# Expert routing formed tile by tile inside the output projection, and the last down weights split into another buffer

## The reference, cut to what matters

```python
x = x + merged @ w_o
h = rms_norm(x, norm2_g)
g_logits = h @ w_group_router + b_group_router      # 4 groups
e_logits = h @ w_expert_router + b_expert_router    # 4 x 8 experts
grp = argmax(g_logits); top_val, top_idx = top_k(e_logits[grp], 2)
gates = softmax(g_logits)[grp] * softmax(top_val)
# tokens sorted by expert, each expert's list padded to blocks of 128 rows
y_block = (silu(xb @ w_gate[e]) * (xb @ w_up[e])) @ w_down[e]
x = x + gates[0] * y[first] + gates[1] * y[second]
y_out = rms_norm(x, final_norm_g)
```

## Time and profile before

| | us |
|---|---|
| median of 3 runs | 1621.45 (1621.17 to 1624.1) |
| the profiled execution, its own time | 1620.94 |
| its span | 1619.1 |
| TensorE busy in the span | 1495.6 (92%) |
| VectorE busy | 931.2 (58%) |
| ScalarE busy | 796.5 (49%) |
| GpSimd busy | 384.5 (24%) |
| the chain that ended last: TensorE | 40% |

### The profile page before, as it was taken

One profiled execution on the slowest core, in us unless ns is written; L12 is line 12 of the kernel. 1 busy time (PEld: TensorE's weight loads), 2 busy tenths in 40 slices (PEclk: granted clock), 3 DMA queues, 4 the chain that ended last, 5 costly groups with the idle time before them and its releaser, 6 DMA issues. The chain is left out here.

```text
span 1619.1 us, 26480 instructions
## 1 busy us (share of the span) xinstructions
PE 1495.6 (92%) x8989; PEld 1316.9 (81%) x8990; DVE 931.2 (58%) x1017; ACT 796.5 (49%) x1040; POOL 384.5 (24%) x403
## 2 busy tenths in 40 slices
PE   5899999999999999998993499999999999999964
PEld 5798998899999899997882388888888888888851
DVE  4415323622335345474336588898886676679836
ACT  4217415712932222551113078878876575677833
POOL 0370073046042000000004333332332222232210
PEclk9999999999999999999996699999999999999987
DMA  6211221232162663464623289999996696699948
GB/s 207 77 62 37 67 81 48 68 93 80 47 220 77 206 134 118 156 207 139 210 92 114 74 313 366 367 380 378 378 389 244 252 385 252 235 366 377 359 174 318
DMA packets 165361, 329.94 MB, mean 204 GB/s; under 512 B 17022, under 2 KB 62376, under 8 KB 164776
## 3 DMA queue, kind: packets, MB, share of 16 engines
q1 hardware_dynamic: 151416, 300.20, 52.9%
q0 software_dynamic: 11568, 20.28, 3.7%
q10 hardware_dynamic: 2304, 8.46, 1.3%
HBM read 300.27 MB, written 49.97 MB: 216 GB/s over the span
## 5 line engine op out<-in xcount | busy, mean ns | idle before, releaser
L2022 DVE TENSOR_TENSOR expert_lo<-expert_raw,expert_hi 128x2048 fp32r<-128x2048 f32 x186 | 416.4, 2289 | 81.9 <-ACT expert_hi L1857 81.9
L1857 ACT CAST expert_hi<-expert_raw 128x2048 fp32r<-128x2048 f32 x192 | 354.7, 1905 | 36.5 <-issue 18.0
L707 PE MATMUL psum<-w_hi,h_T_hi 128*128 128x256 f32 (+1 forms) x792 | 230.3, 291 | 4.4 <-DVE w_lo L563 2.4
L2133 PE MATMUL psum<-expert_hi,block_T_hi 128*128 128x512 f32 x576 | 228.6, 397 | 2.3 <-DVE block_T_lo L2035 2.3
L2133 PE MATMUL psum<-expert_hi,block_T_lo 128*128 128x512 f32 x576 | 225.5, 392 | 0.0
L2133 PE MATMUL psum<-expert_lo,block_T_hi 128*128 128x512 f32 x576 | 225.0, 391 | 0.0
L707 PE MATMUL psum<-w_hi,h_T_lo 128*128 128x256 f32 (+1 forms) x792 | 223.7, 282 | 0.0
L707 PE MATMUL psum<-w_lo,h_T_hi 128*128 128x256 f32 (+1 forms) x792 | 223.7, 282 | 0.0
L707 PEld LDWEIGHTS psum<-w_hi,h_T_hi 128*128 128x128 f32 (+1 forms) x792 | 141.5, 179 | 11.9 <-issue 6.4
L707 PEld LDWEIGHTS psum<-w_lo,h_T_hi 128*128 128x128 f32 (+1 forms) x792 | 141.6, 179 | 2.7
L707 PEld LDWEIGHTS psum<-w_hi,h_T_lo 128*128 128x128 f32 (+1 forms) x792 | 141.5, 179 | 2.8
(11 more groups left out here) (281 smaller groups left out, 2781.5 us busy)
## 6 DMA issues: line engine op xcount, KB each, us to landing
expert_raw<-in_w_gate_dram SPq DMA_DIRECT2D x64, 1024.0 KB, 9.3
expert_raw<-in_w_up_dram SPq DMA_DIRECT2D x64, 1024.0 KB, 7.7
expert_raw<-in_w_down_dram SPq DMA_DIRECT2D x64, 1024.0 KB, 8.9
w_raw<-in_w_in_dram SPq DMA_DIRECT2D x21, 1024.0 KB, 5.8
gate_logits<-gate_logits_out ACTq DMA_DIRECT2D x16, 516.0 KB, 2.8
gate_logits_even<-gate_logits SPq DMA_DIRECT2D x8, 516.0 KB, 4.1
gate_logits_odd<-gate_logits SPq DMA_DIRECT2D x8, 516.0 KB, 4.6
x_in<-in_x_prompt_dram SPq DMA_DIRECT2D x8, 512.0 KB, 5.3
```

What stands on the lines that cost most here:

```text
L707: m = nc.tensor.matmul(dst, st, mv, start=(k == 0 and n == 0), stop=(k == KD - 1 and n == 2))
L1857: nc.scalar.copy(weh[:, u], wraw[:, SLOT[u]]).then_inc(s_uh[m], 1)
L2022: nc.vector.tensor_tensor(wel[:, u], wraw[:, SLOT[u]], weh[:, u].bitcast(F32), ALU.subtract).then_inc(s_ul[m], 1)
L2133: m = nc.tensor.matmul(bank(m_), x_, w_, start=(u == 0 and k == 0 and i == 0), stop=(u == 1 and k == 3 and i == 2))
```

## The change

Routing moves into the w_o stage, and the two `Block`s and the barrier between them become one. TensorE turns the residual rows themselves (`x_mixed`) and not the normed ones: the router weights are multiplied by the norm's gain once (`s_wr`), and the logits are scaled by the row's inverse root when they are read. The turning of tile t-1 and its router product stand inside the products of tile t. The root's sum of squares goes from VectorE to ScalarE (`root`). VectorE chooses the experts of tile t-1 (`choose`, 17 operations of at most 36 columns) and places those of tile t-2 (`place`, 7 operations); TensorE gets two rank products a tile (`ranks`). After the last tile only blocks per expert, first blocks and the table remain.

The routing's tiles now stand in the memory of two halves of `expert_raw`, those of the down weights. SyncE therefore waits for the slot table (`s_tb`) before it loads the first down weights; the order of its queue stays as it was. GpSimd's `split_first` is gone: VectorE forms all low parts, those of the first down weights in the body of block 1. The first two gathers read their index column from the table without a copy. The owner table is counted by TensorE. The last down weights are split into the gate weights' place (`weh[:, 0:2]`, `wel[:, 0:2]`) and multiplied from there, and the down product of block 34 is cut in two around `hidden_T`. The test for the second block of a pair stands inside that for the first.

```diff
 (w_o stage, VectorE)
+                def choose(t):
+                    r = rows(t)
+                    dve.wait_ge(s_rt, t + 1)
+                    V.scalar_tensor_tensor(logits[0:r, t, :], bank(6)[0:r, 0:36], rstd[0:r, t:t + 1], brr[0:r, :],
+                                           ALU.mult, ALU.add).then_inc(s_lg, 1)
...
+                def place(t):
+                    r = rows(t)
+                    dve.wait_ge(s_rn, t + 1)
+                    V.tensor_tensor(trk[0:r], oh[0:r, :, t, :],
+                                    rank_bank(t)[0:r, 0:NE].unsqueeze(1).to_broadcast([r, 2, NE]),
+                                    ALU.mult).then_inc(s_rr, 1)
...
+                for t in range(TILES):
+                    if t + 1 < TILES:
+                        tile_lo(t + 1)
...
+                    add_rows(t)
...
+                    if t:
+                        choose(t - 1)
+                    inverse_root(t)
+                    if t < NT:
+                        normed(t)
+                    if t >= 2:
+                        place(t - 2)
+                choose(NT)
+                place(NT - 1)
+                dve.wait_ge(s_tot, 1)
...
+                place(NT)
+                normed(NT)
+                dve.wait_ge(s_fe, 1)
 (w_o stage, TensorE)
+                for t in range(TILES):
+                    pe.wait_ge(s_mtl, t + 1)
+                    if t >= 2:
+                        pe.wait_ge(s_x2, 2 * (t - 1))
+                    products(t, 0, range(KD))
+                    if t:
+                        rows_turned(t - 1)
+                    products(t, 1, range(KD // 2))
+                    if t:
+                        router(t - 1)
+                    products(t, 1, range(KD // 2, KD)).then_inc(s_wop, 1)
+                    if t >= 2:
+                        ranks(t - 2)
+                rows_turned(NT)
+                router(NT)
+                ranks(NT - 1)
+                ranks(NT)
 (SyncE)
+                sp.wait_ge(s_tb, 1)
                 for u in range(4, UN):
                     load_half(sp, u, 0)
                 load(1, range(UN))
 (GpSimd)
-                split_first(range(4))
...
-                    if not later(b, 1):
-                        split_first(range(4, UN))
 (VectorE, body of a block)
                 def body(b, even, odd):
+                    split_lo(0, b)
                     if later(b, 1):
-                        split_lo(0, b)
                         hidden(b - 1)
                     rows_lo(b)
+                    split_lo(1, b)
                     if later(b, 1):
-                        split_lo(1, b)
                         hidden_lo(b - 1)
-                    if later(b, 2):
                         split_lo(2, b - 1)
+                    else:
+                        block_table()
+                        gates()
 (all engines, the loop)
-                for odd in range(2):
-                    with eng.If(b + odd < n):
-                        body(b + odd, b, odd)
+                with eng.If(b < n):
+                    body(b, b, 0)
+                    with eng.If(b + 1 < n):
+                        body(b + 1, b, 1)
 (ScalarE and TensorE after the loop)
+                for u in range(2):
+                    act.wait_ge(s_ui[4 + u], 16 * NE)
+                    nc.scalar.copy(weh[:, u], wraw[:, SLOT[4 + u]]).then_inc(s_lh, 1)
...
-                down(last2)
+                down(last2, [0])
                 hidden_T(last2 + 1)
-                down(last2 + 1)
+                down(last2, [1])
+                down(last2 + 1, last=True)
```

More of the change, by code:

```diff
@@ new lines, in add_rows @@
+                def add_rows(t):
+                    r = rows(t)
+                    dve.wait_ge(s_wop, t + 1)
+                    dve.wait_ge(s_xi[t % 2], 16 * (t // 2 + 1))
+                    if t >= 2:
+                        dve.wait_ge(s_x2o[t % 2], 16 * (t // 2))
+                        dve.wait_ge(s_h2T, t - 1)
+                    for half in range(2):
+                        cols = slice(512 * half, 512 * half + 512)
+                        nc.vector.tensor_tensor(x2[0:r, t % 2, cols], bank(2 * (t % 2) + half)[0:r, :],
+                                                xo[0:r, t % 2, cols], ALU.add).then_inc(s_x2, 1)
@@ new lines, in rows_turned, with router @@
+                def rows_turned(t):
+                    r = rows(t)
+                    pe.wait_ge(s_x2, 2 * (t + 1))
+                    if t:
+                        pe.wait_ge(s_h2c, 2 * t)
+                    for k in range(KD):
+                        m = nc.tensor.transpose(bank(4 + k // 4)[:, (k % 4) * P:(k % 4) * P + r],
+                                                x2[0:r, t % 2, k * P:(k + 1) * P], ident[0:r, 0:r])
+                    m.then_inc(s_h2T, 1)
+                def router(t):
+                    r = rows(t)
+                    pe.wait_ge(s_h2c, 2 * t + 2)
+                    if t == 0:
+                        pe.wait_ge(s_wr, 1)
+                    if t:
+                        pe.wait_ge(s_lg, t)
+                    for k in range(KD):
+                        m = nc.tensor.matmul(bank(6)[0:r, 0:36], h2T[:, t % 2, k, 0:r], wr[:, k, :],
+                                             start=(k == 0), stop=(k == KD - 1))
+                    m.then_inc(s_rt, 1)
@@ L2109, in _ @@
                 m.then_inc(s_tm, 1)
+                pe.wait_ge(s_cmo, 1)
+                nc.tensor.matmul(bank(7)[0:1, 0:NBMAX], cone[0:NE, 0:1], cmpo[:], start=True, stop=True) \
+                    .then_inc(s_own, 1)
                 def rows_T(b, buf):
@@ L2143, in hidden_T, with down @@
                     m.then_inc(s_hT7, 1)
-                def down(b):
-                    e = expert_of(pe, b)
-                    pe.wait_ge(s_tl, b + 1)
-                    if later(b, 1):
-                        pe.wait_ge(s_y, 2 * b)
-                    for u in range(2):
-                        pe.wait_ge(s_ul[2], 2 * e + 1 + u)
+                def down(b, halves=range(2), last=False):
+                    if not last:
+                        e = expert_of(pe, b)
+                    if 0 in halves:
+                        pe.wait_ge(s_tl, b + 1)
+                        if later(b, 1):
+                            pe.wait_ge(s_y, 2 * b)
+                    for u in halves:
+                        if last:
+                            pe.wait_ge(s_ll, u + 1)
+                        else:
+                            pe.wait_ge(s_ul[2], 2 * e + 1 + u)
+                        at = u if last else 4 + u
                         for k in range(2):
```

574 lines of the change are left out of this document (288 added, 286 removed).

## The result

The changed kernel takes 1605.9 us (median of 4 runs, 1603.9 to 1607.75) and the kernel before, on the same chip, 1621.92 us: a ratio of 0.9899, 95% interval 0.9882 to 0.9916. The forecast was 1595.5 us. The direction and the places came out as forecast; the gain is some 10 us smaller.

The account below looks back on a forecast made before the run. TensorE bounds the expert loop, loads close behind; a chain of small VectorE operations fills the hole before it. 1620.94 less 15.9 (kept at block 2's end) less 9.5 (tail) gave 1595.5 us; range 1582 to 1608.

Parts of the forecast that it names:

- dear small operations: Rival: VectorE's 63 small operations on the chain cost 0.40 us each, not 0.23; 10.7 us more, 1606.2 us; chance 0.14.
- The w_o stage grows: w_o stage on TensorE: 6.8 us more work ahead of the last product, VectorE's last add at 862.7 us, not 855.86.
- the chain shrinks: VectorE, last w_o add to slot table: 22.8 us, with 59 small operations at 0.23 us; table at 885.5 us.
- The table products: Before the slot table: the second choice's nine TensorE products cost 0.17 to 0.34 us each, taken as 2.3 us.
- From table to first product: Slot table to first gate product: gather 2.67, landing 2.02, then 3.46 us, with hand-over 8.3 us; product at 893.8 us.
- the lock between the two engines: First gather: VectorE and GpSimd shut each other out of SBUF; gather ends 1 us later than taken, total 1596.5 us.
- The wait in block 2: Third block: gate 2 queues behind down 1, TensorE idles 9.9 us and restarts at low clock; price 12.4 us, once.
- no-starvation: Rival: gate 2's weights come in time for block 2, so its 12.4 us price goes; 1583.1 us; chance 0.13.
- The loop: Expert loop after block 2: keeps its work, 33 blocks cost the same as before.
- A lost head start: Rival: without weights loaded ahead, loads run late each block until an expert's second block; 4 to 8 us; chance 0.10.
- a loop bound by its loads: Rival: loads under 362 GB/s lose the whole gain; at 350 GB/s the loop takes 46 us more, 1641 us; chance 0.03.
- The tail: Last up product to end of last down product: 15.7 us, not 25.2; gain 9.5 us; what follows moves as a whole.

## Why the prediction was right in direction and 10 us off in size

The stated range of 1582 to 1608 us holds the measured 1605.9 us; the forecast's own, 1590 to 1601, does not. The wider one reaches so far up because of dear small operations, which did not come, so that it held is partly luck. Two steps on the way to the first product, and a smaller one at the end, were mis-sized.

- **The w_o stage grows, the chain shrinks.** Right: no waits of TensorE inside the tiles, last add 0.9 us later than forecast, small operations at 0.24 us. (The terms of a tile add up to 14.2 us and not to 13.9; the turnings of two tiles stand 14.1 us apart. The sum doesn't use it.) The rival of dear small operations gave 1606.2 us, which is the measured time by accident only: its 0.40 us each are not there.
- **The table products: the step that failed first.** "The nine products of the second choice cost between 0.17 and 0.34 us each, since 18 of twice the columns took 6.15 us at the low clock" was read from one merged row without its clock. They cost 0.44 us at 1.2 GHz. The first choice's nine also no longer fit beside VectorE's 1.7 us for the second, so the second nine start late: from the second choice's one-hot rows to the last product 6.26 us and not 2.3. That is 4.0 of the 4.1 us; the run with added products gave the price at 2.4 GHz.
- **From table to first product: the second step.** "2.02 us to land" came from a gather with idle DMA engines. The change puts down 0's load, which had long been done, and gate 1's behind the same table, and so beside the gather: 5.36 us, 3.3 us more; holding the loads back brought 3.0 us. Another 0.8 us is GpSimd's 0.98 us from the table to the gather's start: I took 0.15, though the brackets of the earlier trace rows show 0.94 and 0.83 us. With T for the table, the gather ended at T + 3.6 us; I had taken T + 2.8, and the lock between the two engines gave T + 3.9.
- **The wait in block 2.** Right, by place, cause and price: 8.83 us against 9.9, and 29.5 - 17.7 = 11.8 us in all against 12.4. Undoing the order gave 11.2 us. So no-starvation falls as well. That the three blocks together come within 0.15 us of the forecast is partly luck: the first takes 12.9 us and not 13.5, the second 14.6 and not 13.5, since TensorE waits 1.67 us for `hidden` there, which was not forecast.
- **The loop.** Right: 583.6 us for 33 blocks in both kernels, 378 GB/s from 1000 to 1200 us. A lost head start and a loop bound by its loads fall.
- **The tail.** Right to 0.3 us as far as it was worked out. "What follows moves as a whole" was wrong: the scatter of block 34 starts in the midst of the last loads, takes 4.8 us to land after GpSimd is done with it (1.76 before, beside few loads), and its buffer is the one that block 35's copy needs. So the last scatter starts 3.0 us after the last down product and not 2.0. This 1.0 us the second buffer gave back; the other 0.9 of the 1.9 us lies in the final stage, within what it differs from one execution to the next. That the loads make the scatter land late is not shown: no run took them away.

## What to carry to other kernels

A duration read from a row belongs to the state in which it was taken: look up the granted clock and what the DMA engines moved in that window before it enters a sum, and ask what the change starts at the same moment. When a table, a flag or a buffer is moved, list everything that it releases; here one table released a gather and the 4 MB that slowed it. And a gain at the start of a loop is worth nothing until the next thing in line is as early: beside the queue's new order the 4 us by which the high clock brought the first product forward paid only once the block table and gate 1 had been moved too.

## What was not expected of the hardware

- In the rows read here an indirect gather or scatter lands 1.8 to 2.2 us after GpSimd is done with it where the DMA share is 0.07 to 0.19, and 4.8 to 6.4 us after it beside loads, where the share is 0.55 to 1.02. That the loads are the reason is shown for the first gather alone.
- An fp32 product with 128x128 weights takes 0.44 us at 1.2 GHz with 48 and with 96 columns, and 0.22 to 0.23 us at 2.4 GHz.
- Products that nothing reads, put into idle stretches, brought 6.4 us by the medians, of which 3.8 are found in the profiled executions up to the end of the third block: the granted clock was 1.00 from 870 to 886 us, where it is 0.50 without them.
- TensorE was busy for the 7.91 us of the table products in the changed kernel, after mostly idling, and stayed at 0.50; in the kernel before, it had idled for 22 us ahead of them, and the clock rose about 4 us into them (0.50 up to 910.0 us, 1.00 from 910.5 us). Why in one and not in the other was not tried.
